# Feed-forward products: tokens in parts of 256 and 288, and one 512-column product for the first part's high and low columns

## The reference, cut to what matters

```python
x = x + 0.5 * rmsnorm(f1, ffn1_post_g)     # f1 = swiglu(rmsnorm(x), ...)
x = x + rmsnorm(y, mix_post_g)             # y = token_mixing(rmsnorm(x), ...)
x = x + 0.5 * rmsnorm(f2, ffn2_post_g)     # f2 = swiglu(rmsnorm(x), ...)

def swiglu(x, w_gate, w_up, w_down):       # 1024 -> 2816 -> 1024, float32
    return (silu(x @ w_gate) * (x @ w_up)) @ w_down
```

## Time and profile before

| | |
|---|---|
| median of three runs | 1175.18 us |
| lowest, highest | 1169.48, 1175.3 us |
| span of the profiled execution | 1167.8 us |
| TensorE busy, matmul records | 1120.6 us (96%), 9522 |
| VectorE, ScalarE busy | 615.3 us (53%), 329.2 us (28%) |
| mean granted TensorE clock | 0.964 of full speed |
| 7632 matmuls of 272 columns (line 306) | 290 to 293 ns a record |
| DMA | 91.99 MB, 79 GB/s, queue 1 busy 25% |

### The profile page before, as it was taken

How to read it: one execution, slowest core, us unless ns; L and a number is a source line. 1 busy time by engine, 2 the same in 40 slices (tenths; PEclk the granted TensorE clock), 3 DMA queues, 4 the chain that set the end, 5 groups by cost and what they waited for, 6 DMA issues and landing times. The chain is left out here.

```text
span 1167.8 us, 22671 instructions
## 1 busy us (share of the span) xinstructions
PE 1120.6 (96%) x9522; PEld 1097.9 (94%) x9522; DVE 615.3 (53%) x1015; ACT 329.2 (28%) x496; POOL 42.9 (4%) x57
## 2 busy tenths in 40 slices
PE   6999999999999999999899989999999999999996
PEld 6999999999999999999777789999999999999996
DVE  5534344323434778788869637873434333243446
ACT  5321222112222334331234433442122221122221
POOL 0000000000000000030223000000000000000001
PEclk9999999999999979999779989899999999999998
DMA  6322323222232221232601002213232322222222
GB/s 216 95 80 90 108 72 103 78 90 91 72 108 72 73 86 38 63 88 60 96 2 39 2 1 93 73 41 95 77 113 72 108 72 90 90 82 98 72 73 77
DMA packets 35394, 91.99 MB, mean 79 GB/s; under 512 B 10368, under 2 KB 12928, under 8 KB 35328
## 3 DMA queue, kind: packets, MB, share of 16 engines
q1 hardware_dynamic: 34320, 88.78, 25.0%
q10 hardware_dynamic: 1008, 2.27, 0.6%
HBM read 87.76 MB, written 3.28 MB: 78 GB/s over the span
## 5 line engine op out<-in xcount | busy, mean ns | idle before, releaser
L306 PE MATMUL ps<-xh,wh 128*128 128x272 f32 x1840 | 404.0, 293 | 16.4 <-DVE xl L503 8.6
L306 PE MATMUL ps<-xh,wl 128*128 128x272 f32 x1840 | 400.3, 291 | 0.0
L306 PE MATMUL ps<-xl,wh 128*128 128x272 f32 x1840 | 399.3, 290 | 0.0
L306 PEld LDWEIGHTS ps<-xh,wh 128*128 128x128 f32 x1840 | 299.3, 191 | 19.0 <-DVE wl L289 9.0
L306 PEld LDWEIGHTS ps<-xl,wh 128*128 128x128 f32 x1840 | 299.6, 191 | 0.0
L306 PEld LDWEIGHTS ps<-xh,wl 128*128 128x128 f32 x1840 | 297.7, 191 | 0.0
L284 ACT ACTIVATE wh<-raw 128x1024 fp32r<-128x1024 f32 (+1 forms) x163 | 168.1, 1034 | 324.6 <-PE ps L306 208.6
L289 DVE TENSOR_TENSOR wl<-raw,wh 128x1024 fp32r<-128x1024 f32 (+1 forms) x163 | 192.8, 1203 | 38.0 <-ACT wh L284 37.7
L306 PE MATMUL ps<-hh,wh 128*128 128x272 f32 x704 | 157.7, 290 | 0.0
L306 PE MATMUL ps<-hh,wl 128*128 128x272 f32 x704 | 156.7, 290 | 0.0
L306 PE MATMUL ps<-hl,wh 128*128 128x272 f32 x704 | 156.5, 289 | 0.0
(11 more groups left out here) (312 smaller groups left out, 790.3 us busy)
## 6 DMA issues: line engine op xcount, KB each, us to landing
raw<-in_w_gu SPq DMA_DIRECT2D x88, 512.0 KB, 3.6
raw<-in_w_d SPq DMA_DIRECT2D x32, 512.0 KB, 3.6
raw<-in_w_in SPq DMA_DIRECT2D x19, 512.0 KB, 3.6
raw<-in_w_d SPq DMA_DIRECT2D x16, 384.0 KB, 3.0
raw<-in_w_out SPq DMA_DIRECT2D x8, 512.0 KB, 3.6
out_y<-x SPq DMA_DIRECT2D x16, 136.0 KB, 1.7
x<-in_x ACTq DMA_DIRECT2D x4, 272.0 KB, 5.6
x<-in_x SPq DMA_DIRECT2D x4, 272.0 KB, 6.7
```

Source lines behind the costliest of these rows:

```text
L306: last = pe.matmul(out[:, n], left[:, s, j], right[:, j, n * H:n * H + H], start=first and opens and j == order[0], stop=final and closes ...
```

## The change

The parts become 256 and 288 tokens. xh and xl become two slices of one tensor `xhl` (low first), hh and hl of `hhl`. The first part's sum stands in the upper half of the pair's first bank (columns 256 to 511), the second part's in the second bank, so that 544 columns lie in one piece and `pair` is one slice.

With `apart`, the first part's wh x xh and wh x xl are one matmul of 512 columns: its moving operand is the low slice followed by the high slice, and the low columns land in the bank's lower half (0 to 255), the high in the upper. wl x xh adds to the upper half. The two halves are added afterwards: ScalarE copies the lower half to SBUF (`low_act`), VectorE adds it (`fold_dve`), into PSUM or, for a down unit of groups 2 and 3, into f. `apart` is on for all feed-forward units but the last four down units of each, and for the first part of the first four units of the second feed-forward. It is off in the mixing. Over the program that makes 992 steps with one matmul less, and 128 units with one copy and one addition more. Six small matmuls of 16 columns that spread the roots over partitions go too, since 256 is two tiles of 128.

```diff
-H = N // 2
-HP = NP_ - H
+H = 256
+WIDE = (H, N - H)
         def pair(n):
-            return ps[:, 2 * n:2 * n + 2, 0:H]
+            return ps[:, 2 * n:2 * n + 2].rearrange("p a b -> p (a b)")[:, 512 - H:512 - H + N]
+        def part_out(n, h):
+            return ps[:, 2 * n + 1, 0:N - H] if h else ps[:, 2 * n, 512 - H:512]
+        def part_low(n):
+            return ps[:, 2 * n, 0:H]
@@ product
-                for left, right in ((wh, right_h), (wh, right_l), (wl, right_h)):
-                    first, final = left is wh and right is right_h, left is wl
-                    for n in parts:
-                        last = pe.matmul(out[:, n], left[:, s, j], right[:, j, n * H:n * H + H], start=first and opens and j == order[0],
-                                         stop=final and closes and j == order[-1])
+                small, big = right[:, 0, j], right[:, 1, j]
+                for left, moving in ((wh, big), (wh, small), (wl, big)):
+                    start, stop = first and left is wh and moving is big, final and left is wl
+                    for h in parts:
+                        if apart and h == 0 and moving is small:
+                            continue
+                        if apart and h == 0 and left is wh:
+                            pe.matmul(ps[:, 2 * n].rearrange("p (k n) -> p k n", k=2), wh[:, s, j], right[:, :, j, part_of(0)],
+                                      start=start, stop=final, skip_group_check=True)
+                            continue
+                        last = pe.matmul(part_out(n, h), left[:, s, j], moving[:, part_of(h)], start=start, stop=stop,
+                                         skip_group_check=apart)
@@ new
+        def low_act(act, q, i, k):
+            act.wait_ge(S("unit_done"), i * 4 + (q * FFN2 + k + 1 + SPL))
+            act.wait_ge(S(f"fold{q}"), i * 4 + (k + 1))
+            act.activation(low[:, k % 2], part_low(k % 4), ACT.Copy).then_inc(S(f"low{q}"), 1)
+        def fold_dve(dve, q, i, k, to=None):
+            dve.wait_ge(S(f"low{q}"), i * 4 + (k + 1))
+            to = part_out(k % 4, 0) if to is None else to
+            return dve.tensor_tensor(to, to, low[:, k % 2], ADD).then_inc(S(f"fold{q}"), 1)
@@ hidden_dve
-            dve.tensor_tensor(halves(silu[:, s % 2]), pair(2 * (s % 2)), halves(rb[:]), MUL).then_inc(S(f"gate{q}"), 1)
+            fold_dve(dve, q, i, k)
+            folded(dve, q, i, k)
+            dve.tensor_tensor(silu[:, s % 2], pair(2 * (s % 2)), rb[:], MUL).then_inc(S(f"gate{q}"), 1)
             unit_done(dve, u, i, 2 * s + 1)
+            fold_dve(dve, q, i, k + 1)
+            folded(dve, q, i, k + 1)
@@ ffn_act, the down units
                     split_hi(act, u, 0, s, nf)
+                    if s < 3 or g < 2:
+                        low_act(act, q, 0, u - u0 + s - 3)
+                    if g == 2 and 2 <= s < 6:
+                        low_act(act, q, 0, u - u0 + s - 2)
```

More of the change, by code:

```diff
@@ L296, in unit_done, with product @@
             eng.wait_ge(S("unit_done"), i * 4 + (u0 + s + 1 + SPL))
-        def product(pe, out, s, order, right_h, right_l, before=None, opens=True, closes=True, parts=(0, 1)):
+        def product(pe, n, s, order, right, before=None, opens=True, closes=True, parts=(0, 1), apart=False):
             for j in order:
@@ L332, in spread_root_pe @@
                 k, j = divmod(t, 3)
-                wide = P if j < 2 else H - 2 * P
-                last = pe.matmul(ps[:, 6 + k, P * j:P * j + wide], st[:, 2, t:t + 1].to_broadcast([P, P]),
+                wide = P if j < 2 else WIDE[k] - 2 * P
+                if not wide:
+                    continue
+                last = pe.matmul(part_out(3, k)[:, P * j:P * j + wide], st[:, 2, t:t + 1].to_broadcast([P, P]),
                                  ident[:, P - wide:P], start=True, stop=True)
@@ L572, in ramp_pe @@
                         split_ready(pe, u, 0, s)
-                    product(pe, pair(s), s, (j,), xh, xl, opens=j == 0, closes=j == KD - 1, parts=(0,))
+                    product(pe, s, s, (j,), xhl, opens=j == 0, closes=j == KD - 1, parts=(0,), apart=n == 3)
                 if j == 2:
@@ L580, in ramp_pe @@
                     split_ready(pe, u, 0, 3)
-                    product(pe, pair(3), 3, range(5), xh, xl, closes=False, parts=(0,))
+                    product(pe, 3, 3, range(5), xhl, closes=False, parts=(0,), apart=n == 3)
                 if j > 4:
-                    product(pe, pair(3), 3, (j,), xh, xl, opens=False, closes=j == KD - 1, parts=(0,))
+                    product(pe, 3, 3, (j,), xhl, opens=False, closes=j == KD - 1, parts=(0,), apart=n == 3)
                 if j == 5:
@@ L751, in ffn_pe @@
                         pe.wait_ge(S(f"d_out{q}"), dn + s + 1)
-                        product(pe, pair(s), s, range(KD), xh, xl).then_inc(S("unit_done"), 1)
+                        product(pe, s, s, range(KD), xhl, apart=True).then_inc(S("unit_done"), 1)
                 u += 2 * nf
@@ L774, in ffn_pe @@
                         pe.wait_ge(S(f"d_out{q}"), i * 4 + (dn + s + 1))
-                        product(pe, pair(s), s, range(nf), hh, hl, hidden_ready if s == 0 else None
+                        product(pe, s, s, range(nf), hhl, hidden_ready if s == 0 else None, apart=True
                                 ).then_inc(S("unit_done"), 1)
@@ L1471, in q_pe @@
                     for n in range(2):
-                        last = pe.matmul(bank(("b", 0), n)[:, 0:H], ones, yb[:, p, n * H:n * H + H], start=p == 0, stop=p == 1)
+                        last = pe.matmul(part_out(1 - side(("b", 0)), n), ones, yb[:, p, part_of(n)], start=p == 0, stop=p == 1)
                 last.then_inc(S("b_mean"), 1)
@@ L1629, in mixer_pe @@
                         for n in range(2):
-                            last = pe.matmul((A, B)[p][:, n], lora_w[rows, P * p:P * p + P],
-                                             (lo if m == 5 else lo2)[rows, n * H:n * H + H], start=True, stop=True)
+                            last = pe.matmul(part_out(2 + p, n), lora_w[rows, P * p:P * p + P],
+                                             (lo if m == 5 else lo2)[rows, part_of(n)], start=True, stop=True)
                         last.then_inc(S("lora"), 1)
@@ L1650, in mixer_pe @@
                         for n in range(2):
-                            last = pe.matmul((A, B)[p][:, n], hb, bo[:, p, n * H:n * H + H], start=True, stop=True)
+                            last = pe.matmul(part_out(2 + p, n), hb, bo[:, p, part_of(n)], start=True, stop=True)
                         last.then_inc(S("bo_sum"), 1)
@@ L1658, in mixer_pe @@
                         for n in range(2):
-                            last = pe.matmul((A, B)[p][:, n], dwbd[:, p], yd[:, p, n * H:n * H + H], start=True, stop=True)
+                            last = pe.matmul(part_out(2 + p, n), dwbd[:, p], yd[:, p, part_of(n)], start=True, stop=True)
                         last.then_inc(S("d_map"), 1)
@@ L1698, in mixer_pe @@
                 for n in range(2):
-                    last = pe.matmul(pair(2 + p)[:, n], hb, yc[:, p, n * H:n * H + H], start=True, stop=True)
+                    last = pe.matmul(part_out(2 + p, n), hb, yc[:, p, part_of(n)], start=True, stop=True)
                 last.then_inc(S("c_mean"), 1)
```

104 lines of the change are left out of this document (60 added, 44 removed).

## The result

The changed kernel takes 1181.78 us (median of 14 runs, 1170.02 to 1188.23), the kernel before, on the same chips, 1172.83 us (14 runs, 1165.08 to 1179.2). The ratio is 1.0081 with an interval of 1.0054 to 1.0109: slower by 0.8%, where 1170.0 us and a ratio of 0.996 were forecast. A later repetition gave 1.0064 (1.0035 to 1.0094).

The account below looks back on a forecast made before the run. TensorE's matmul pace was taken to bound the kernel. Terms -11.0 - 0.6 + 4.0 + 1.4 + 1.0 = -5.2 us, from 1175.18 to 1170.0 us (chance 0.62); own range 1165 to 1175, 8-in-10 range 1158 to 1181.5.

Parts of the forecast that it names:

- point 1: Feed-forward steps: one matmul less saves a fixed 11.7 ns in each of 944 steps, -11.0 us.
- The point at which the change would begin to lose: Feed-forward steps: a saving of 5 ns a step, below which the change was said to lose.
- The rival that the extra time goes with the columns: Feed-forward steps: 512 columns take 235 ns, the step stays at 750 ns, only costs remain, 1181.0 us; chance 0.17.
- The load as the pace: Feed-forward steps: the weight load sets the pace, 715 ns a step, 32 us saved, 1148 us; chance 0.10.
- The jump between the slices: 512-column matmul: moving operand might stream slower between slices, 5 ns each, 5 us, 1175 us; chance 0.11 shared with costlier seams.
- Point 2: Spreads of the roots: six small 16-column matmuls, twelve records, go; -0.6 us.
- Point 3: Feed-forward loops: added copies on ScalarE and additions on VectorE are hidden, costed at nothing.
- Point 4: End of the first feed-forward: a copy ahead of unit 6's high part delays the sums, +4.0 us, bounds 2.5 and 5.
- Point 5: Start of the second feed-forward's loop: copies and additions enter the chain to gate and up, +1.4 us, bounds 0.8 and 2.
- Point 6: After the two longer waits: 2.5 us more of low clock, costing 1.0 us, bounds 0 and 6.

Follow-up runs that it names:

- e1: Changed kernel plus matmul streams of one width after the last spread; 118.3 ns for 256 columns, 125.0 for 272, 133.3 for 288, 230.0 for 512.
- e3: Changed kernel with the 512-column matmul made as two of 256, copies and additions kept; ratio 1.0069 to the kernel before, 749 ns a step.
- e5: Changed kernel plus isolated streams of mixed-width steps in several orders (W 512 columns; h, l, v 288; w 256); 740.0 to 753.1 ns per five-product step in six orders.
- e6: Changed kernel plus isolated streams, 24 cyclic orders of its five products and 28 of six 272-column ones; 744.8 to 753.4 and 747.2 to 756.7 ns a step.
- e7: Changed kernel with the 288-column product of wl ahead of the 256-column one; ratio 1.0002 to the kernel before, 744.6 ns a step.
- e8: Changed kernel with both 288-column products of wh ahead of the 512-column one; ratio 0.9961 to the kernel before, 741.3 ns a step.
- e9: e7 without lower halves in the last down group's first four units and the second feed-forward's first two; 1167.98 us, ratio 0.9943 to the kernel before.
- e11: e8 without lower halves in the last down group's first four units and the second feed-forward's first two; 1163.8 us, ratio 0.9921 to the kernel before.
- e12: Changed kernel measured again, unaltered; 1182.54 us, ratio 1.0064 to the kernel before.
- e2: Changed kernel's parts of 256 and 288 and its layout alone, six products a step, no copy or addition; ratio 0.9993 to the kernel before.
- e10: Kernel before with its two 272-column parts taken in the order 0 1, 1 0, 1 0; ratio 1.0010 to the kernel before.

## Why the prediction was wrong

The step that failed is point 1, the price of one matmul less. It took the 11.7 ns above 272 columns as fixed per pair of load and matmul and saw a step of 738 ns. Measured is 753.2, which is +2.8 instead of -11.7 ns; in 944 steps +2.6 instead of -11.0 us. These 13.6 us are as much as the whole miss (forecast -5.2, measured +7.5 to +9.5 us). Two things were wrong in it. In an even stream only 6.7 ns are fixed and the rest goes with the columns, so a merging saves 6.6 ns (e1). And prices do not add: by e1's the five products would take 748 ns and the six of e3 755, and they take 753 and 749. In the order W h l w v the five settle in a rhythm that gives back more than the merging saves (e3, e5, e6), in two other orders they are faster than 748 (e7, e8). Why a rhythm has its length is open. The trace of before had one width and one order and could show neither. Its low clock has nothing above the columns, and that argued for neither form. The point at which the change would begin to lose was also mis-added: costs of 5.8 us in 944 steps are 6.1 ns a step, not 5. The bounds of the terms add up to 1166 to 1176 us, not 1165 to 1175.

The rival that the extra time goes with the columns came out at the right time, 1181.0 us, for a reason that is half right. Its 235 ns for the wide product were 232.8 in the loop, but 230.0 in the even stream, and by it e7 and e8 could not exist. The load as the pace falls: a pair of load and product takes 112 ns at 64 columns and 118 at 256, so whatever is fixed in a pair, the load or another thing, is a floor of some 112 ns and not the pace above it. The jump between the slices falls by e1.

Point 2, the spreads, is too small to be told apart. Point 3, copies and additions in the loops, stands: 383 ns a copy and 432 or 425 an addition, where the earlier trace rows gave 384 and 406, and no wait in any loop:

```profile
L804 DVE TENSOR_TENSOR ps<-ps,low 128x256 f32<-128x256 f32 x104 | 45.0, 432 | 288.9 <-ACT low L798 288.9
...
L798 ACT ACTIVATE low<-ps 128x256 f32<-128x256 f32 x128 | 49.0, 383 | 404.1 <-PE ps L320 404.1
```

Point 4, the first seam, was right link by link: f of unit 3 at 396.22, 4.7 us after the copy's start at the unit's end (5.1 forecast), waits of 0.52 and 4.69 us against 1.62, so +3.6 us for 4.0. Point 5 as well: 3.6 against 2.4 us, +1.2 to 1.3 for 1.4. Taking both seams out gave 0.6% (e7 to e9) and 0.4% (e8 to e11), 7 and 5 us, each uncertain by 0.4%; the waits alone had grown by 4.9 us.

Point 6, the clock, was about right. The share of the clock that is missing is half the share of time at 1.2 GHz, so a mean clock lower by 0.001 is 2.3 us more at that level, 0.9 us at the 0.4 us that each costs. The profiled executions alone make the term look larger: 0.960, 0.963, 0.964, 0.962 and 0.962 in the five kernels with both long seams (changed, e12, e3, e7, e8), 0.964, 0.969, 0.964, 0.966 and 0.966 in the five without (before, e2, e9, e10, e11), which would be 3.4 us; but one kernel's executions range over as much. Over all executions, e3, e7, e8 and e12 have 0.0030, 0.0019, 0.0006 and 0.0005 less than the kernel before beside them (12 executions of each, against 18 to 35). That is 0.0015 in the mean, 1.4 us, where 1.0 was put in.

Pace 2.6, spreads -0.6 (forecast, not measured), seams 4.9 and clock 1.4 make 8.3 us, beside 7.5 to 9.5 measured. One term stood in no point of the prediction, TensorE's wait for s0t. It is some 3 us longer in the traces of five products. With it the sum is 11 us, which the intervals of the two comparisons (4 to 13 us) still allow.

## What to carry to other kernels

Where TensorE is full, a matmul has no price of its own: measure a whole step of mixed widths, in each order that the sums allow, before its pace goes into a forecast, and then in the kernel, since a stream by itself can settle otherwise. Fewer and wider matmuls can be slower; in the kernels here five products took 741 to 753 ns by their order, six took 749 to 750. A copy that waits for TensorE, put into a queue that also carries the next weights, was free in the loops and cost 3.6 and 1.3 us at the two seams where its chain ended last, so leave it out there.

## What was unexpected

Streams of 64 and then 128 columns let the clock fall while TensorE was never idle. The window in e1:

```profile
1188.00:1208.00 20.00, 20.00 (x96) 20.00 (x95) 0.00 (x0) 0.00 (x0) 0.00 (x0) 0.50 0.00 1
```

There a product of 64, one of 128 and one of 256 columns each took 213 ns, so the floor of 112 ns at the full clock is about twice as high at the low one. Each product has a load of its own in these streams, and no run shows which of the two sets the floor.

TensorE's wait for s0t, an input of the mixing, was 0.3, 2.1, 1.3 and 1.9 us in the four kernels with six products (before, e10, e2, e3) and 2.6 to 5.4 us in the ten traces of those with five; the means are 1.4 and 4.4. The transfer landed 11 to 15 us after its issue. Nothing of it was touched. The wait is not hidden. From the first sums to the start of the second loop the traces of the changed kernel take 383.4 and 383.1 us (e12), that of the kernel before 375.3. In the first of them what stands ahead of the wait takes 175.6 us in place of 174.8, the wait is 4.7 us longer, and what stands behind takes 202.8 in place of 200.2, with the second seam in it. That e11, the fastest, has the longest wait only says that it could be faster still. Whether chance or something of the change sets it stays open, as does what makes the rhythms.
